# Two ordinary gate and up tiles instead of four, parts of 8, 6 and 8 tiles, and another schedule for the weight-sum transfers

## The reference

```python
mixed = gate_a * (o_a @ w_branch_a[l]) + gate_b * (o_b @ w_branch_b[l])
h = h + mixed @ w_out[l]
hn = rms_norm(h, ffn_norm_g[l])
h = h + (jax.nn.silu(hn @ w_ffn_gate[l]) * (hn @ w_ffn_up[l])) @ w_ffn_down[l]
```

## Time and profile before

| | |
|---|---|
| median of 3 runs | 1513.41 us |
| lowest, highest | 1510.56, 1517.55 us |
| the profiled execution | 1518.73 us, span 1517.0 us |
| TensorE clock granted, mean | 0.987 |
| PE busy | 1474.9 us (97%) |
| DVE, ACT, POOL busy | 980.3, 654.1, 257.8 us |
| HBM | 233.48 MB read, 81.88 MB written |

### The profile page before, as it was taken

How to read it: one execution, slowest core, us unless ns; L and a number is a source line. 1 busy time by engine, 2 the same in 40 slices (tenths; PEclk the granted TensorE clock), 3 DMA queues, 4 the chain that set the end, 5 groups by cost and what they waited for, 6 DMA issues and landing times.

```text
span 1517.0 us, 23810 instructions
## 1 busy us (share of the span) xinstructions
PE 1474.9 (97%) x8700; PEld 1264.4 (83%) x8700; DVE 980.3 (65%) x1779; ACT 654.1 (43%) x1175; POOL 257.8 (17%) x260
## 2 busy tenths in 40 slices
PE   9999998878999999999999999999999999999998
PEld 8868885656889899989889877777777898998997
DVE  6678976544577568668864274342766774875776
ACT  4235445512535246336521165444344542552554
POOL 2023445310110000000001555334111011000000
PEclk9999999988999999999989999999999999999999
DMA  7535576688799266356223303237899989953642
GB/s 170 151 102 175 167 130 167 153 166 214 212 193 241 84 185 189 100 160 180 77 80 87 84 14 98 93 102 126 262 224 202 250 256 211 271 159 109 182 124 98
DMA packets 342910, 236.92 MB, mean 156 GB/s; under 512 B 24730, under 2 KB 322838, under 8 KB 342815
## 3 DMA queue, kind: packets, MB, share of 16 engines
q1 hardware_dynamic: 305518, 152.24, 35.1%
q0 software_dynamic: 37216, 83.27, 24.3%
q10 hardware_dynamic: 80, 0.14, 0.0%
HBM read 233.48 MB, written 81.88 MB: 208 GB/s over the span
## 4 chain that ended last, share of the span: by engine, by line
PE 83%; DMA 7%; DVE 5%; ACT 2%; issue 1%; POOL 0%; DVEq 0%; SPq 0%; ACTq 0%; POOLq 0%
PE psL L2288 29%; PE psS L2311 12%; PE psL L2515 12%; PE psL L2311 7%; PE psS L2288 5%; PE psT L2311 5%; DMA stage<-in_w_branch_a 4%; PE psT L2524 2%; DMA stage<-in_w_branch_b 2%; DVE wl L1393 1%; PE psS L2831 1%; ACT wh L913 1%; PE psS L2565 1%; PE psL L2786 1%; DMA stage<-in_w_out 1%
## 5 line engine op out<-in xcount | busy, mean ns | idle before, releaser
L913 ACT ACTIVATE wh<-stage 128x1024 fp32r<-128x1024 f32 (+3 forms) x211 | 203.4, 964 | 404.6 <-PE psL L2288 192.1
L1393 DVE TENSOR_TENSOR wl<-stage,wh 128x1024 fp32r<-128x1024 f32 (+2 forms) x168 | 184.0, 1095 | 86.8 <-ACT wh L913 86.4
L2288 PE MATMUL psL<-hid,wh 128*128 128x512 f32 x680 | 210.5, 391 | 0.7 <-DVE wl L1393 0.6
L2288 PE MATMUL psL<-hn,wh 128*128 128x512 f32 x528 | 165.2, 394 | 0.6 <-DVE wl L1393 0.6
L2515 PE MATMUL psL<-hn,wh 128*128 128x512 f32 x496 | 165.0, 414 | 0.2 <-DVE yn L2171 0.2
L2288 PEld LDWEIGHTS psL<-hid,wh 128*128 128x128 f32 x680 | 126.6, 188 | 29.2 <-DVE wl L1393 2.6
L2288 PE MATMUL psL<-hid,wl 128*128 128x512 f32 x340 | 132.3, 389 | 0.0
L747 POOL TENSOR_TENSOR wl<-stage,wh 128x1024 fp32r<-128x1024 f32 (+1 forms) x43 | 97.6, 2272 | 179.4 <-ACT wh L913 179.4
L2288 PEld LDWEIGHTS psL<-hn,wh 128*128 128x128 f32 x528 | 97.6, 188 | 24.0 <-issue 3.3
L2515 PEld LDWEIGHTS psL<-hn,wh 128*128 128x128 f32 x496 | 84.5, 189 | 23.9 <-issue 11.0
L2288 PE MATMUL psL<-hn,wl 128*128 128x512 f32 x264 | 102.9, 390 | 0.0
(11 more groups left out here) (507 smaller groups left out, 3375.3 us busy)
## 6 DMA issues: line engine op xcount, KB each, us to landing
stage<-in_w_in SPq DMA_DIRECT2D x53, 512.0 KB, 3.8
wsum<-weight_sums_1g SPq DMA_DIRECT2D x18, 512.0 KB, 4.6
wsum<-weight_sums_1u SPq DMA_DIRECT2D x18, 512.0 KB, 4.3
wsum<-weight_sums_2g SPq DMA_DIRECT2D x18, 512.0 KB, 5.0
wsum<-weight_sums_2u SPq DMA_DIRECT2D x18, 512.0 KB, 4.9
stage<-in_w_out SPq DMA_DIRECT2D x16, 512.0 KB, 4.9
stage<-in_w_ffn_down SPq DMA_DIRECT2D x32, 256.0 KB, 2.9
stage<-in_w_ff_down SPq DMA_DIRECT2D x32, 256.0 KB, 3.0
```

The costliest lines, as they stand in the source:

```text
L913: act.activation(wh[:, b, 0:n], stage[:, b, 0:n], ACT.Copy).then_inc(hi[b], 1)
L1393: v.tensor_tensor(wl[:, b, 0:n], stage[:, b, 0:n], wh[:, b, 0:n].bitcast(F32), ALU.subtract).then_inc(lo[b], 1)
L2288: ins = pe.matmul(dst, w[:, b, k * P:(k + 1) * P], x[:, part, k, c0:c1], start=done_ + n == 0, stop=done_ == kc - 1 and n == 2)
```

## The change

1. `FPARTS` becomes 8, 6, 8, and `GATE_PLAIN` 2, 0, 0. Two ordinary gate and two ordinary up tiles become two entries of `pair_list` in each layer. Entries by part are 6, 6 and 8 instead of 4, 8 and 6; the columns of a weight-sum DMA are 384, 384 and 512.
2. The four token sums, spread over four ordinary tiles before, are all made within two, and the first weight-sum half and the second weight half are converted behind them.
3. In the first entry of part a PE's half products come in the order x, x1, z, y instead of x, y, x1, x, z.
4. SP waits for the fourth token sum only ahead of the `wsum` loads, no longer ahead of the first pair's weights.
5. POOL's DMAs: in part b only n = 0, 8, 12, 14 wait. `feed_sums` holds the rest (part b from n = 8, all of part c) until the first token sum of the layer is made. In layer 2, `SUMS_AT[2]` puts all sixteen of part a and the first eight of part b between the gate products.

```diff
-FPARTS = (8, 8, 6)
+FPARTS = (8, 6, 8)
-GATE_PLAIN = (4, 0, 0)
+GATE_PLAIN = (2, 0, 0)
-SUMS_AT = (0, 2, 3, 4, 5, 6, 8, 12, 14)
+SUMS_AT = {1: (0, 2, 3, 4, 5, 6, 8, 12, 14), 2: (0, 4, 8, 12, 12, 14, 16, 20, 24)}
@@ load_pair (SP)
                 load(name, i, 0, w, pair * P)
+                sp.wait_ge(xt_sum, 4 * l)
                 if q:
@@ layer_rest (SP)
-                    if part == 0:
-                        sp.wait_ge(xt_sum, 4 * l)
@@ sum_dmas (POOL)
-                    if before + n and (n in (0, 8, 12, 14) or (l, part) not in ((1, 0), (2, 0))):
+                    if before + n and (n in (0, 8, 12, 14) or part == 2):
@@ POOL's order
+            def feed_sums(l):
+
+                pool.wait_ge(xt_sum, 4 * l - 3)
+                sum_dmas(l, 1, 8, SUM_DMAS)
+                sum_dmas(l, 2, 0, SUM_DMAS)
...
-            sum_dmas(1, 1, 8, SUM_DMAS)
-            sum_dmas(1, 2, 0, SUM_DMAS)
+            feed_sums(1)
...
-                sum_dmas(2, 0, SUMS_AT[i], SUMS_AT[i + 1])
-            sum_dmas(2, 0, 14, SUM_DMAS)
-            sum_dmas(2, 1, 0, SUM_DMAS)
-            sum_dmas(2, 2, 0, SUM_DMAS)
+                part = SUMS_AT[2][i] // SUM_DMAS
+                sum_dmas(2, part, SUMS_AT[2][i] - part * SUM_DMAS, SUMS_AT[2][i + 1] - part * SUM_DMAS)
+            feed_sums(2)
@@ swiglu (ACT)
-                    if i < 2:
-                        token_sum_high(l, i)
-                    elif i == 2:
-                        token_sum_high(l, 3)
+                    token_sum_high(l, i)
                     if i < plain - 1:
                         high(name, i + 1, 1)
                     else:
+                        token_sum_high(l, 2)
+                        token_sum_high(l, 3)
+                    inner_high(i, part, f0)
+                    if i == plain - 1:
                         sum_high(entries[0][1], 0)
                         second_high(name, entries[0][0])
@@ tile_pair (PE)
-                pe.wait_ge(ws_lo, 2 * q + 1)
-                pe.wait_ge(xt_lo, 4 * l)
-                half_product(y, mixed, 0, token_sums(0)).then_inc(acc_y, 1)
-                half_product(x1, first, SEQ, rows_of(KD // 2, 0)).then_inc(mm[0], 1)
+                if part == 0 and e == 0:
+                    half_product(x1, first, SEQ, rows_of(KD // 2, 0)).then_inc(mm[0], 1)
+                    pe.wait_ge(lo[1], PAIR0[name] + i + 1)
+                    pe.wait_ge(xt_lo, 4 * l)
+                    half_product(z, second, SEQ, token_sums(3)).then_inc(mm[1], 1)
+                    pe.wait_ge(ws_lo, 2 * q + 1)
+                    half_product(y, mixed, 0, token_sums(0)).then_inc(acc_y, 1)
```

More of the change, by code:

```diff
@@ L806, in _ @@
                     low_pair("gates1", i)
-                sum_dmas(1, 0, SUMS_AT[i], SUMS_AT[i + 1])
+                sum_dmas(1, 0, SUMS_AT[1][i], SUMS_AT[1][i + 1])
             def mask_bias(j):
@@ L1196, in swiglu @@
                     else:
+                        token_sum_high(l, 2)
+                        token_sum_high(l, 3)
+                    inner_high(i, part, f0)
+                    if i == plain - 1:
                         sum_high(entries[0][1], 0)
                         second_high(name, entries[0][0])
-                    if i == 1:
-                        token_sum_high(l, 2)
-                    inner_high(i, part, f0)
                 if not plain:
@@ L1935, in swiglu @@
                         token_sum(l, 1)
[L1936 to L1939, removed]
                     done(name, i, 0)
@@ L1947, in swiglu @@
                         token_sum(l, 2)
-                    elif i == 2:
+                        token_sum_low(l, 1)
                         token_sum(l, 3)
+                    times_up(name, i, f0, ft[:, 0, :], (lambda: low(name, i + 1, 1)) if i < first - 1 else None)
+                    inner_low(i, part, f0)
+                    if i == first - 1:
                         token_sum_low(l, 2)
-                    elif i == first - 1:
+                        token_sum_low(l, 3)
                         sum_low(q0, 0)
                         second_low(name, first)
-                    times_up(name, i, f0, ft[:, 0, :], (lambda: low(name, i + 1, 1)) if i < first - 1 else None)
-                    inner_low(i, part, f0)
                 def product_of(m, inner):
@@ L2333, in tile_pair @@
                 half_product(x, first, 0, rows_of(0, 0)).then_inc(acc_x, 1)
-                pe.wait_ge(ws_lo, 2 * q + 1)
-                pe.wait_ge(xt_lo, 4 * l)
-                half_product(y, mixed, 0, token_sums(0)).then_inc(acc_y, 1)
-                half_product(x1, first, SEQ, rows_of(KD // 2, 0)).then_inc(mm[0], 1)
+                if part == 0 and e == 0:
[5 more added lines that the diff above has]
+                    half_product(y, mixed, 0, token_sums(0)).then_inc(acc_y, 1)
+                else:
+                    pe.wait_ge(ws_lo, 2 * q + 1)
+                    half_product(y, mixed, 0, token_sums(0)).then_inc(acc_y, 1)
+                    half_product(x1, first, SEQ, rows_of(KD // 2, 0)).then_inc(mm[0], 1)
                 pe.wait_ge(out_x, 2 * q + 1)
                 half_product(x, mixed, SEQ, token_sums(1), add=True).then_inc(acc_x, 1)
-                pe.wait_ge(lo[1], PAIR0[name] + i + 1)
-                half_product(z, second, SEQ, token_sums(3)).then_inc(mm[1], 1)
+                if part or e:
+                    pe.wait_ge(lo[1], PAIR0[name] + i + 1)
+                    half_product(z, second, SEQ, token_sums(3)).then_inc(mm[1], 1)
                 pe.wait_ge(ws_lo, 2 * q + 2)
```

## The result

The changed kernel took 1536.60 us (median of 4 runs, 1528.65 to 1541.63), the kernel before 1515.48 (median of 4). The ratio is 1.0144, 95% interval 1.0103 to 1.0186. The forecast was 1511 us, with a range of 1493 to 1524. The profiled execution took 1541.63 us, its span is 1539.9 us.

A forecast was written before the change was run, and what follows sets the result against it. PE, busy 1474.9 of 1517.0 us, was taken as the bound: matmul time, waits and half clock. Terms -34 - 3.2 + 24 + 9 + 1 - 1.5 + 2 = -2.7 on the 1513.4 median gave about 1511 us, range 1493 to 1524.

The forecast's parts named there:

- Transfers beside the tile pairs: First adds of part b go out four at once beside the first tile pairs; late loads cost 2 us (0 to 10).
- sign that I had named of being wrong: Two signs: PE waits at z for less than 5 us, or its idle time stands at the start of part c.
- Rival C: Tile pairs starved of loads while held transfers run, 1 us and more over some six entries a layer: 1523 us; chance 0.09.
- Branch and output products: Without weight-sum transfers beside them, both layers' products leave 2 us over each: gain 34 us (28 to 38).
- Token sums: Part a, sums in half the time: PE idles 10.5 us at z plus clock loss, 24 us in all (15 to 30).
- rival A: Small losses, gain stays: token sums 7.5 to 8.5 us a layer, latent attention 3; 1494 us; chance 0.36 with mixtures.
- Latent attention: Layer 1: part a's transfers of 384 columns, not 256, delay `biasM`; loss 9 us (gain of 4 to loss of 13).
- Matmuls: Two tile-pair entries replace two ordinary rounds in each layer: gain 1.6 us a layer, 3.2 in all.
- Gates of layer 2: Eight copies of 384 columns go out at once before POOL waits at n = 8: cost 1 us (0 to 4).
- Parts of 8, 6 and 8: Last down product gets 24 matmuls, not 18, per product, long enough to hide rounding and split: gain 1.5 us.
- B: Rival: part c's weight sums come too late, PE stands 10 us a layer; 1535 us at worst, 1523 if half; chance 0.11.

The follow-up runs named there:

- transfers alone: The kernel before with only the change's edits to POOL's transfers, keeping parts of 8, 8 and 6 and four ordinary tiles: 1521.6 us, ratio 1.006.

## Why the prediction was wrong, step by step

- *Transfers beside the tile pairs*, forecast +2 (0 to 10), is the step that failed: +48.6, made of 31.4 in the two parts a and 17.2 behind them. I took it from the one stretch in which PE had no idle time, with single adds of 384 columns and four ordinary tiles behind the token sums. That reading was right: transfers alone shows it again in part b. But nothing there bounded several at once, which measured 21.0 us of the 48.6 (106.9 - 99.0 with two in flight in layer 1, 111.3 - 98.3 with four in layer 2), nor single adds beside pairs whose slack the hurried token sums had used up (5.5 and 4.9), nor 1 MB adds beside part b (17.2; as copies they cost it nothing). The range of an unmeasured load should have reached to what the earlier trace rows show: a 256 KB load of 7.7 to 8.8 us beside a single 1 MB add. The branch product lost 33 us to single adds; I let four at once pass for 2.
- The Trainium skill, "DMA: Bandwidth & Descriptors", Queues, rings and completion order, was used to say that four transfers in POOL's queue slow SP's loads no more than one. The traces agree with what the Trainium skill states there, that an engine takes turns between queues by packets (401 against 404). The step from it was wrong: a load has 1024 packets and an add 512, so one add in the queue slows half of a load and two slow all of it, 12.26 us against 7.07.
- Neither sign that I had named of being wrong covers this: PE waited 9.7 and 13.9 us at z, not under 5, and nowhere at the start of part c.
- Rival C had the mechanism and a quarter of its size: 12 us for twelve entries.
- *Branch and output products*, forecast -34: -34.7. The windows are 88.9 and 89.2 us at clock 1.00, as written.
- *Token sums*, +24 forecast (15 to 30): 93.4 - 84.7 = 8.8 and 9.2, 18.0. The wait at z is there, on DVE's split of the second weights, 7.3 us where I had 10.5: the weight sums landed in 3.9 us, not 7, when no held transfer ran beside them. With them it was 9.7 us in layer 1 of the changed kernel:

```profile
PE psS L2309 <- DVE wl L1902: 9.7, 1, 9.7
```

The working itself holds: with a landing of 3.9 it gives 7.4. Without the held transfers it is rival A's size of 8.5 a layer. But this price is only what the sums cost by themselves. Going from four to two ordinary tiles cost 37 us with single adds moved (1481 to 1518). Of that, 24 lie in the parts a, more than the 18 of the sums, since it also makes loads late that ordinary tiles would have hidden, and 11 lie ahead of the branch product (294.1 for 282.7), where the sums of part a are wider. I had treated these terms as independent.
- *Latent attention*, +9 forecast (-4 to 13): +1.6. The three waits ended at 221.5, 233.4 and 244.8 us, not 224.5, 237.5 and 251.5: half as much again on bytes took 1.2 times as long, not 1.5. The price of the wider transfers was right all the same: against transfers alone, where the branch product began at 281.53, it began 12.7 us later, for 13 forecast. What was wrong is the gain of the waits that went, 11.3 us (281.53 against 292.80) and not 4. The largest wait of PE that is left there:

```profile
PE psT L2530 <- ACT W L1051: 6.8, 3, 6.3
```

- *Matmuls*, -3.2: not seen apart; part a has 611 PE instructions for 540, where 72 more were due. *Gates of layer 2*, +1: 0 in the changed kernel, though 5 to 16 us in the three kernels with copies or without held transfers, which my bound of 4 didn't hold.
- *Parts of 8, 6 and 8*, -1.5: -7.3 (5.4 and 1.9). I priced only the last product of layer 2; that of layer 1, ahead of the key-value products, gains more. Alone, this edit gave 14 us, mostly by narrower adds beside the branch product, which the full change no longer had to gain.
- B did not happen: no wait stood at part c. Its 1535 us are near the measured time by chance.

Sum: -34.7 + 1.6 - 3.2 + 18.0 + 48.6 - 7.3 + 0 = 23.0, measured 22.9. I was 46.6 us too low in one term and 20.9 too high in the others together.

Not settled: why POOL's issue stood at the third add in layer 1 and not in layer 2, and how much of part a's loss comes from each load that landed late.

## What to carry over

A wait between background transfers is a throttle: before taking it away, measure the foreground loads beside one and beside several, since a row with one in flight says nothing of four. Count packets to see how far: a load is slowed for as long as packets stand in the other queue. Slack ahead of a tight stage (ordinary tiles) and bandwidth beside it are the same resource, so don't spend both in one change. Move background work to where each load has most time, not only out of the stage that suffers: holding it over the branch product alone took 20.6 us off that stage (109.1 to 88.5) and cost 0.9 in parts a and b.

## What the runs showed of the hardware

- While both have work, POOL's queue and SP's take turns one for one by packets: 401 against 404 (adds of 1536 B rows), 256 against 259 (copies). A packet took 139 ns for 1536 B added, 82 ns for 768 B added, 217 ns for a copy's of 4.2 KB in the mean, 41 ns for SP's 512 B beside adds and 27 ns alone.
- The packets of adding transfers from DRAM to DRAM took 93 engine-us per MB in the changed kernel, those of copies 45.
- Transfers in a row on POOL's queue: the fourth issue stood for 9.24 us (copies) and 12.77 us (adds), with the engine's other work behind it; in the changed kernel the third add stood for 11.73. Each went out 0.2 to 0.5 us after all before it had landed. Yet four adds of 768 KB went out without standing at 1158.01 us. What sets this was not tried.
- With the clock granted at 0.89 to 0.92 in part a of the changed kernel, PE is busy for 89 us there, and for 86 with a clock of 0.96 and no held transfers: 3 us a layer of the loss are clock, behind its idle times.
